# Two decoder blocks on one core: the last quarter of the gate products, one weight load and several VectorE steps in another order

## The reference

```python
mod = silu(c) @ w_ada + b_ada                       # 2048 -> 6 * 2048
shift_m, scale_m, gate_m, shift_f, scale_f, gate_f = split(mod, 6)
h = rms_norm(x, pre_norm_mix) * (1 + scale_m) + shift_m
q_n, k_c, v_c, k_s, v_s, k_w, v_w, g_n, q_m, k_m, v_m = split(h @ w_in)
gates = sigmoid(g_n)                                # 8 heads x 3 branches
kc, vc = compress(rope(k_c)), compress(v_c)         # silu(blocks @ w1) @ w2
o_n = gates[0] * attn(q, kc, vc) + gates[1] * attn(q, k_s, v_s) + gates[2] * attn(q, k_w, v_w)
o_m = attn(rope(q_m), rope(k_m), v_m)
x = x + gate_m * rms_norm(concat(o_n, o_m) @ w_o)
x = x + gate_f * rms_norm(relu(h2 @ w_up)**2 @ w_down)
```

## Time and profile before

| | |
|---|---|
| median of 3 runs | 2943.92 us (2943.36 to 2948.78) |
| the profiled execution | 2948.24 us |
| its span, first to last instruction | 2946.4 us |
| TensorE busy | 2879.6 us, 98% |
| VectorE busy | 1684.6 us, 57% |
| ScalarE busy | 1266.2 us, 43% |
| GpSimd busy | 105.2 us, 4% |
| moved by DMA | 596.74 MB, mean 203 GB/s |

### The profile page before, as it was taken

The page is one execution under the profiler, slowest core; times in us unless marked ns, Lnnn a source line. Parts: engine busy times, 40 slices in busy tenths (PEclk is TensorE's granted clock), DMA queues, the critical chain, the costliest instruction groups (busy, mean ns, idle before and its releaser), DMA issues.

```text
span 2946.4 us, 51149 instructions
## 1 busy us (share of the span) xinstructions
PE 2879.6 (98%) x22398; PEld 2654.8 (90%) x22398; DVE 1684.6 (57%) x1503; ACT 1266.2 (43%) x1238; POOL 105.2 (4%) x95
## 2 busy tenths in 40 slices
PE   6999999999999999999999999999999999999999
PEld 5999998899889997899999889999889998899888
DVE  7879788784444454465455654445745544445544
ACT  3334554445334443345344544444345443344433
POOL 0010000000000000000012410000000000000000
PEclk8799999999999999999999999999999999999999
DMA  9999878596556665655451015656555655565553
GB/s 356 385 318 331 278 248 318 182 356 201 193 188 198 189 197 177 204 186 172 149 177 56 10 51 195 197 188 228 172 186 162 196 189 197 187 198 189 183 187 127
DMA packets 300501, 596.74 MB, mean 203 GB/s; under 512 B 12192, under 2 KB 17824, under 8 KB 299808
## 3 DMA queue, kind: packets, MB, share of 16 engines
q1 hardware_dynamic: 294912, 587.83, 59.5%
q10 hardware_dynamic: 5408, 6.23, 0.8%
HBM read 583.80 MB, written 6.29 MB: 200 GB/s over the span
## 4 chain that ended last, share of the span: by engine, by line
PE 88%; DVE 5%; DMA 3%; ACT 3%; issue 1%; POOL 0%; SPq 0%; ACTq 0%; DVEq 0%
PE ps L2452 29%; PE ps L2375 26%; PE ps L2989 9%; PE ps L2559 6%; PE ps L2574 3%; PE ps L3112 2%; DVE wL L1392 2%; PE ps L2870 2%; DMA raw<-w_up 2%; PE ps L2533 1%; DVE ada_acc L1612 1%; ACT wH L777 1%; DMA ada<-w_ada 1%; PE ps L2498 1%; PE ps L2398 1%
## 5 line engine op out<-in xcount | busy, mean ns | idle before, releaser
L1392 DVE TENSOR_TENSOR wL<-raw,wH 128x2048 fp32r<-128x2048 f32 x436 | 1002.6, 2300 | 1069.6 <-ACT wH L777 1065.3
L777 ACT ACTIVATE wH<-raw 128x2048 fp32r<-128x2048 f32 x436 | 838.0, 1922 | 1323.4 <-PE ps L2452 460.5
L2452 PE MATMUL ps<-actH,wH 128*128 128x256 f32 x2816 | 780.0, 277 | 3.1 <-DVE wL L1392 2.9
L2452 PE MATMUL ps<-actL,wH 128*128 128x256 f32 x2816 | 777.8, 276 | 0.0
L2452 PE MATMUL ps<-actH,wL 128*128 128x256 f32 x2816 | 777.7, 276 | 0.0
L2452 PEld LDWEIGHTS ps<-actH,wH 128*128 128x128 f32 x2816 | 528.9, 188 | 6.1 <-DVE wL L1392 3.2
L2452 PEld LDWEIGHTS ps<-actL,wH 128*128 128x128 f32 x2816 | 529.0, 188 | 0.1
L2452 PEld LDWEIGHTS ps<-actH,wL 128*128 128x128 f32 x2816 | 528.9, 188 | 0.0
L2375 PE MATMUL ps<-wH,hidH 128*128 128x512 f32 x1024 | 403.4, 394 | 1.3 <-DVE wL L1392 1.3
L2375 PE MATMUL ps<-wH,hidL 128*128 128x512 f32 x1024 | 400.4, 391 | 0.0
L2375 PE MATMUL ps<-wL,hidH 128*128 128x512 f32 x1024 | 397.4, 388 | 0.0
(11 more groups left out here) (444 smaller groups left out, 3639.5 us busy)
## 6 DMA issues: line engine op xcount, KB each, us to landing
raw<-w_in SPq DMA_DIRECT2D x96, 1024.0 KB, 5.7
ada<-w_ada SPq DMA_DIRECT2D x80, 1024.0 KB, 8.3
raw<-w_up SPq DMA_DIRECT2D x64, 1024.0 KB, 5.4
raw<-w_down SPq DMA_DIRECT2D x64, 1024.0 KB, 5.2
raw<-w_mlp_up SPq DMA_DIRECT2D x64, 1024.0 KB, 5.3
raw<-w_mlp_down SPq DMA_DIRECT2D x64, 1024.0 KB, 5.0
raw<-w_gates SPq DMA_DIRECT2D x48, 1024.0 KB, 5.1
raw<-w_o SPq DMA_DIRECT2D x16, 1024.0 KB, 7.5
```

Of the source, the lines that this page charges most:

```text
L777: nc.scalar.activation(wH[:, s % SPLIT if L[name]["spg"] > 1 else r % SPLIT, :, :], raw[:, slot, :, :], ACT.Copy).then_inc(wh_ready, 1)
L1392: nc.vector.tensor_tensor(wL[:, b, :, :], raw[:, slot, :, :], wH[:, b, :, :].bitcast(F32), ALU.subtract).then_inc(wl_ready, 1)
L2452: ins = nc.tensor.matmul(out, w[:, b, k, cols], v[:, kk, :], start=(kk == 0 and j == 0 and n % 2 == 0), stop=(kk == STEP_K * spg - 1 and j ...
```

## The change

It keeps all computations. It moves: on TensorE the last quarter of the gate products from the end of front to behind (0,3); on SP weight block 15 (the one of step (0,3)) ahead of the second 2 MB of the compression weights; on VectorE the low part of (0,1) ahead of the first rotation, and so the later ones too, modulation block 34 behind (1,1), 35 between the two halves of the third rotation, the first maximum, and blocks 40 and 41 from ahead of the first softmax weights to behind (2,0); on ScalarE the sigmoid of the gates to behind (1,1), and a copy of value tokens ahead of `take_pT(6)`.

```diff
-    WIN_ADA = [(2, 0, 0, 1), (1, 1, 3, 4), (1, 1, 0, 1)] + [(2, 1, 0, 1)] * 4 + [(2, 1, 0, 4)]
+    WIN_ADA = [(0, 1, 1, 1), (1, 1, 3, 4), (1, 1, 0, 1)] + [(2, 1, 0, 1)] * 4 + [(2, 1, 0, 4)]
@@ SP
             sp.dma_start(cw1[:, 0, :, :], a["cmp_k_w1"].rearrange("(l d) h -> d l h", d=P)).then_inc(cmp_in, 16)
+            weight_block(11 + RAW)
             sp.dma_start(cw1[:, 1, :, :], a["cmp_v_w1"].rearrange("(l d) h -> d l h", d=P)).then_inc(cmp_in, 16)
             sp.dma_start(cw2[:, 0, :], a["cmp_k_w2"]).then_inc(cmp_in, 16)
             sp.dma_start(cw2[:, 1, :], a["cmp_v_w2"]).then_inc(cmp_in, 16)
-            weight_block(11 + RAW)
@@ ScalarE
             swap_halves(1)
-            act.wait_ge(gate_done, 1)
-            nc.scalar.activation(gate[:, :, :], ps[:, 7, 0:TT * GATES].rearrange("p (t g) -> p t g", t=TT),
-                                 ACT.Sigmoid).then_inc(gate_ready, 1)
             split("w_in", 0, 0, 2)
...
             split("w_in", 0, 1, 1)
+            act.wait_ge(gate_done, 1)
+            nc.scalar.activation(gate[:, :, :], ps[:, 7, 0:TT * GATES].rearrange("p (t g) -> p t g", t=TT),
+                                 ACT.Sigmoid).then_inc(gate_ready, 1)
             split("w_in", 0, 1, 2)
...
             exps(7)
+            v_tokens(4, 5)
             take_pT(6)
             split("w_o", 0, 0, 1)
-            v_tokens(4, 5)
             weigh(7)
@@ VectorE
             ada_blocks(1)
+            split("w_in", 0, 0, 1)
             rope(0)
-            split("w_in", 0, 0, 1)
+            split("w_in", 0, 0, 2)
             compress_inputs()
-            split("w_in", 0, 0, 2)
+            split("w_in", 0, 0, 3)
             rope_sin(1)
             rope_sum(1)
-            split("w_in", 0, 0, 3)
+            split("w_in", 0, 1, 0)
+            split("w_in", 0, 1, 1)
             ada_blocks(1)
-
-            split("w_in", 0, 1, 0)
-            ada_blocks(1)
-            split("w_in", 0, 1, 1)
             rope_sin(2)
             ada_blocks(1)
             rope_sum(2)
             split("w_in", 0, 1, 2)
-            ada_blocks(3)
+            ada_blocks(2)
+            mask_max(0)
+            ada_blocks(1)
             modulation(8, 3)
             split("w_in", 0, 1, 3)
-            mask_max(0)
-            ada_blocks(2)
+            ada_blocks(1)
             dve.wait_ge(gate_ready, 1)
             weights_of(0)
...
             split("w_in", 0, 2, 0)
-            ada_blocks(2)
+            ada_blocks(4)
@@ TensorE
-                ins = gate_part(c)
-            ins.then_inc(gate_done, 1)
+                if c < 3:
+                    gate_part(c)
...
             w_in_step(0, 3)
+            gate_part(3).then_inc(gate_done, 1)
```

## The result

The changed kernel takes 2948.69 us (median of 14 runs, 2942.71 to 2955.89), the kernel before, run beside it, 2944.05 (14 runs, 2941.13 to 2948.84). The ratio is 1.0018, its 95% interval 1.0011 to 1.0025: 3 to 7 us slower, which is clear of the scatter, though at 0.18% no more than the 0.2% that the forecast took for the least that can be told. It is 1.8 us above the forecast of 2946.9. The profiled execution of the changed kernel took 2950.21 us.

A forecast was written before the change was run, and what follows sets the result against it. TensorE, busy 98% of the span, bounds the kernel, so only its work or gaps matter. Terms -0.5, +3.9, +0.1 and -0.45 sum to +3.0 us, from 2943.92 to 2946.9; range 2940.5 to 2950.3.

The forecast's parts named there:

- Part 1: Last gate quarter behind (0,3) covers ScalarE's copy: step (1,0) 1.9 us earlier, 0.5 left if the clock falls again.
- rival sum: At the moved gate products: the clock dip may vanish, and the sum would be 1.4 us lower.
- Part 2: Weight block 15 ahead of the second half of the compression weights: costs nothing; without it the (0,3) stall grows by 2.
- Part 3: Later modulation blocks on VectorE: TensorE waits 2.9 to 4.9 us ahead of (2,1), taken as 3.9.
- slot chain: Between low parts of (2,0) and (2,1): blocks 40, 42, 44 share two slots, each landing following a use; TensorE waits 2.9 us.
- GpSimd collision: GpSimd's rotation may meet VectorE's block 42 ahead of (2,1): 2.0 us longer if it hits, half of it counted.
- C: End of step (1,2) on TensorE, 227.36 us in the earlier trace; (2,1) is wanted at C + 21.7.
- the rival at 0.15: A stall of 4.9 us at (2,1) brings the clock down, another 1.4 to 1.6; sum +5.6, chance 0.15.
- Part 4: First softmax weights and mask earlier, gate sigmoid later: both free nothing on TensorE, 0.
- Part 5: Last value tokens ahead of the transposed weights: values(6) 1.05 us earlier, 0.45 left after waiting for ScalarE's weighing.
- The rival that the late blocks don't bind: VectorE keeps its lead over (2,1), only the gains remain: -0.95 to -3.7 us, 2940.2 to 2943.0; chance 0.30.
- the one that nothing was binding: The gap closes but TensorE waits for the same thing a step later; time stays at 2943.9 us, chance 0.08.

The follow-up runs named there:

- one block back: The changed kernel with modulation block 40 alone back ahead of the modulation and first softmax weights: 2946.24 us (one run).
- the moved transfer: The changed kernel with the transfer of group 1's turned halves for the fourth rotation issued behind the high part of (2,2), four steps later: 2946.37 us (one run).
- the late blocks alone: The kernel before with one edit, modulation blocks 40 and 41 moved behind (2,0): 2955.44 us (5 runs), ratio 1.004.

## Why the prediction was right, and where its sizes were off

**Part 1, -0.5.** Right in sum and mechanism: -0.55 at the scores. The wait for the copy is gone, (1,0) starts 1.81 us earlier by the lag (forecast 1.9), the clock falls behind the 24 products in their new place, and (0,3) waits 0.92 (forecast 0.7). VectorE's low part for it took 4.45 beside GpSimd, as the earlier trace rows. But the sum is not stable. In four profiles of kernels with the same code up to the scores the gain was 0.51 to 0.65, and in two (one block back, the moved transfer) 1.69, with the same fall of the clock in all six. In those two the meeting went the other way, the low part of (0,3) took 2.3, GpSimd's rotation 5.9 to 6.2, and (0,3) didn't wait:

```profile
173.90 6.16 POOL L2263 TENSOR_TENSOR proj<-proj,c 128x1024 f32<-128x1024 f32 x1 [7.67 <-DMA swap_q<-proj]
174.33 2.31 DVE L1394 TENSOR_TENSOR wL<-raw,wH 128x2048 fp32r<-128x2048 f32 x1
```

The forecast had only the loss on VectorE's side. That the fall behind the 24 products isn't certain, as it said with its rival sum, shows in the kernel with weight block 15 back, where they stand in one piece and the clock stayed at 1.00. The Trainium skill (TensorE: Matmul & The Clock Gate, What's actually happening) says that the gate's window runs freely; that the same products can go either way agrees with it, and no run here shows when the window begins.

**Part 2, nothing, and 2 if undone.** The nothing is right. The 2 doesn't follow from the forecast's own rows: a landing at 176.5, 1.9 and 2.2 give 180.6, against the 180.5 that VectorE's queue sets there anyway. Measured, the wait is 0.75 and 1.84 longer when undone, and whether that costs time in sum stays open.

**Part 3, +3.9 of 2.9 to 4.9.** 4.70, within the bounds, by the slot chain that the forecast described. Two steps in it are wrong. The landing was taken as 5.4 for every block, from two landings of the earlier trace rows with no other transfer beside them; block 43 took 9.28. And the GpSimd collision, costed at half of 2.0, cost nothing: the rotation ran from 240.16 for 2.69 us, and VectorE stood idle from 240.6. It came at C + 14.9 and not at C + 11.8, since its own transfer took longer beside the blocks (6.3 us to land, median of its two parts, and 3.5 before). That two errors of opposite sign kept the sum near is luck. The low part of (2,1) ended at C + 26.4, not C + 24.6 (C = 225.26 now). The 0.1 for (2,3) shows nowhere; nothing waits there. Undoing the two blocks took away the whole wait, which shows the cause.

**The clock behind the stall** is the term that was mis-sized: nothing in the sum, 1.77 in the trace. It stood as the rival at 0.15, tied to a stall of 4.9, because the one idle time looked at had 3.76. It fell behind the changed kernel's 1.03 and 3.27, and behind 1.86 alone. With it the sum is -0.55 + 4.70 + 1.77 - 0.34 = +5.6, which is what w_o shows. It is the rival's number too, but by other terms: the rival had the collision in it, which didn't come. The medians differ by 4.6, between the forecast's +3.0 and the rival.

**Part 4, nothing.** No wait of TensorE shows for either edit. But the slot chain starts 2.7 us sooner than with the late blocks alone, by the rows because of the earlier maximum, and without it the price of part 3 would have been larger.

**Part 5, -0.45.** -0.34, and -0.31 alone, with a wait of 0.75 for the weighing where 0.6 was forecast.

The rival that the late blocks don't bind is refuted by the waits, the one that nothing was binding by the gains at the scores.

## What to carry to other kernels

Where two slots are refilled as they are used, postponing the use postpones the next landing by as much, so an idle engine's early work is its lead: look at who waits one group later before moving it. Sum such a chain with the landing as it is beside the other queue's transfers, not with an undisturbed one. When a forecast has TensorE wait 2 us or more behind narrow products, add the 1.2 GHz behind it, 1.6 to 2.4 us here. And where VectorE and GpSimd meet, cost both outcomes: which of the two is held up changed between kernels whose code up to there is the same.

## What the runs showed of the hardware that I had not expected

A 1 MB landing that took 5.3 us alone took 9.28 while 0.5 MB of turned halves moved on a second queue, and 6.81 in another order; for a microsecond its queue moved 0.01 MB beside 0.20. Of a rotation of GpSimd and a low part of VectorE that met near 174 us, now the one took 6.2 instead of 2.4 and now the other 4.5 instead of 2.3. The clock fell behind a wait of 1.86 us that followed one-column products, and not behind one of 1.67 that followed products of 256 columns. The granted clock can stay at 0.50 for some 30 us (213 to 243) though TensorE has no idle time, in a step that runs at 1.00 in another kernel with the same products. An fp32 product of 512 columns with a plain fp32 weight took 0.86 us at 2.4 GHz and shows as two records (10 records, and 4.29 us from the first of 5 products to what follows them).
